# Six norms with fewer sums on TensorE, and another order of a gather's first head, in a two-block decoder kernel

## The reference

```python
def rmsnorm(x, g):
    ms = jnp.mean(xf * xf, axis=-1, keepdims=True)
    return xf * lax.rsqrt(ms + EPS) * g
```

```python
s1, s2 = query_half_1 @ sub_keys1.T, query_half_2 @ sub_keys2.T   # 128 scores each
v1, i1 = top_k(s1, 16); v2, i2 = top_k(s2, 16)
top_s, pos = top_k(v1[:, None] + v2[None, :], 16)                 # 16 of 256 pairs
eidx = i1 * 128 + i2 at pos;  g = softmax(top_s)
a = gelu(expert_down[eidx] . x)                                   # 16 rows of 1024
out += (g * a) @ expert_up[eidx]                                  # 16 rows of 1024
```

## Time and profile before

| what | value |
|---|---|
| median of 3 runs | 1639.43 us (1639.33 to 1641.08) |
| profiled execution, its own time | 1639.54 us |
| its span in the trace | 1637.8 us |
| mean granted TensorE clock | 0.898 of full |
| busy: PE / DVE / ACT / POOL | 81% / 59% / 21% / 30% |
| DMA in the mean | 238 GB/s, 389.75 MB |
| chain that ended last | PE 53%, DMA 26%, DVE 12%, POOL 4% |

### The profile page before, as it was taken

How to read it: one execution, slowest core, us unless ns; L and a number is a source line. 1 busy time by engine, 2 the same in 40 slices (tenths; PEclk the granted TensorE clock), 3 DMA queues, 4 the chain that set the end, 5 groups by cost and what they waited for, 6 DMA issues and landing times.

```text
span 1637.8 us, 14570 instructions
## 1 busy us (share of the span) xinstructions
PE 1332.4 (81%) x5214; PEld 936.5 (57%) x5214; DVE 959.0 (59%) x1851; ACT 338.5 (21%) x677; POOL 493.6 (30%) x390
## 2 busy tenths in 40 slices
PE   7999999999999999999999987565566656555554
PEld 5665668888888888886787776222222222222221
DVE  7799974123311000323412168898988998988977
ACT  2444222321100000122312122111111121111111
POOL 2477670000000000000000024755555555555550
PEclk9999999999999999999999998877777777877776
DMA  6222222244344444322242377999999999999995
GB/s 238 77 78 77 78 103 103 103 157 177 128 149 148 150 145 153 128 103 103 77 143 91 117 303 288 405 422 421 422 422 421 422 422 421 422 422 422 421 422 211
DMA packets 55150, 389.75 MB, mean 238 GB/s; under 512 B 6336, under 2 KB 6656, under 8 KB 8368
## 3 DMA queue, kind: packets, MB, share of 16 engines
q0 software_dynamic: 37488, 271.20, 40.1%
q1 hardware_dynamic: 16560, 115.48, 19.7%
q10 hardware_dynamic: 1040, 2.26, 0.4%
HBM read 387.88 MB, written 1.05 MB: 237 GB/s over the span
## 4 chain that ended last, share of the span: by engine, by line
PE 53%; DMA 26%; DVE 12%; POOL 4%; issue 2%; ACT 2%; ACTq 0%; DVEq 0%
DMA feat<-in_expert,arena 26%; PE psD L930 16%; PE psD L978 7%; PE psD L384 7%; PE psD L881 6%; POOL feat L1782 4%; PE psD L949 3%; PE psD L1288 1%; DVE feat L1795 1%; PE psN L313 1%; DVE arena L619 1%; DVE feat L1829 1%; DVE feat L537 1%; PE psD L874 1%; PE psD L575 1%
## 5 line engine op out<-in xcount | busy, mean ns | idle before, releaser
L930 PE MATMUL psD<-feat,ring 128*128 128x256 f32 (+1 forms) x1248 | 278.1, 383 | 4.4 <-DVE feat L338 3.2
L930 PEld LDWEIGHTS psD<-feat,ring 128*128 128x128 f32 x1248 | 238.6, 192 | 39.1 <-issue 4.5
L1782 POOL DMA_INDIRECT arena<-in_expert,arena x102 | 140.0, 1373 | 208.7 <-DVE arena L1762 53.0
L1970 POOL DMA_DIRECT2D arena<-in_sub x1 | 0.6, 577 | 525.2 <-ACT feat L1504 525.2
L881 PE MATMUL psD<-feat,ring 128*128 128x256 f32 (+1 forms) x576 | 138.1, 396 | 3.0 <-ACT feat L916 3.0
L1795 DVE CUSTOM_DVE_ANT_0 arena<-arena,feat 128x1024 f32<-128x1024 f32 x102 | 120.7, 1220 | 12.8 <-DMA arena<-in_expert,arena 12.8
L881 PEld LDWEIGHTS psD<-feat,ring 128*128 128x128 f32 x576 | 109.2, 194 | 30.5 <-issue 10.5
L1619 PE MATMUL psB<-arena 128*128 128x512 f32 x96 | 73.2, 923 | 64.1 <-ACT arena L1694 64.1
L1782 POOL DMA_INDIRECT feat<-in_expert,arena x77 | 107.7, 1398 | 57.9 <-DVE feat L1829 17.0
L978 PE MATMUL psD<-feat,ring 128*128 128x256 f32 x512 | 111.2, 379 | 0.0
L384 PE MATMUL psD<-feat,ring 128*128 128x256 f32 x512 | 110.8, 379 | 0.0
(11 more groups left out here) (501 smaller groups left out, 2203.1 us busy)
## 6 DMA issues: line engine op xcount, KB each, us to landing
ring<-in_w SPq DMA_DIRECT2D x108, 1024.0 KB, 4.8
arena<-in_expert,arena POOLq DMA_INDIRECT x102, 27.1
feat<-in_expert,arena POOLq DMA_INDIRECT x77, 28.7
feat<-in_xT SPq DMA_DIRECT2D x2, 544.0 KB, 4.6
arena<-in_w_akv POOLq DMA_DIRECT2D x1, 1024.0 KB, 5.2
feat<-in_memT POOLq DMA_DIRECT2D x1, 1024.0 KB, 5.9
out<-feat SPq DMA_DIRECT2D x4, 256.0 KB, 4.7
ring<-in_expert,arena POOLq DMA_INDIRECT x60, 28.7
```

The source lines that it names most:

```text
L930: mm = nc.tensor.matmul(psD[:, 2 * (c % 2) + m, 0:T], ring[:, c % RING, k, m * P:(m + 1) * P], x[:, k], start=(k == 0), stop=(k == KT - 1))
L1782: (nc.gpsimd.indirect_dma_start(GPAIR[b], None, a["expert"], bass.IndirectOffsetOnAxis(ap=EID[:, t, c:c + 1], axis=0)) .then_inc(s_gb[b], 16))
```

## The change

It has three parts.

- **Norms 2 to 7.** `squares_dve(i)` adds, on DVE, the squares of blocks 2 and 3 to those of blocks 0 and 1, and then those of blocks 4 and 5. `sums_pe(i)` is now one call of four matmuls (blocks 0, 1, 6, 7) at the place where the last pair stood; the spread pairs are gone.
- **First head.** Its four calls of `coefficients` move from behind the heads (3, 5, 6, 7) to behind (2, 4, 5, 7). Row i of step 0 takes buffer `SOON[i % 9]` of `[2, 3, 4, 12, 13, 14, 15, 0, 1]`. So (1, 0) to (1, 4) wait for (0, 7) to (0, 11), (1, 5) to (1, 11) for the last scores, (1, 12) to (1, 15) for (0, 12) to (0, 15).
- **Last step.** `both` moves from behind group 2 to behind group 1; group 2's own rows (8 and 10) are added into `ACC` one after the other; `close(1)` also waits for row (15, 10).

```diff
-SOON = 9
+SOON = [2, 3, 4, 12, 13, 14, 15, 0, 1]
...
-    def sums_pe(i, j):
-        nc.tensor.wait_ge(s_sqp, 4 * (i - 2) + j + 1)
-        if j == 0:
-            nc.tensor.wait_ge(s_rt, i)
-        for k in (2 * j, 2 * j + 1):
-            mm = nc.tensor.matmul(psN[:, 0:T2], ones[:, :], SQ[:, k, 0:T2], start=(k == 0), stop=(k == KT - 1))
-        if j == 3:
-            mm.then_inc(s_ms, 1)
+    def squares_dve(i, link):
+        for j in (1, 2):
+            nc.vector.wait_ge(s_sqp, 4 * (i - 2) + j + 1)
+            ins = nc.vector.tensor_tensor(SQ[:, 0:2, 0:T2], SQ[:, 0:2, 0:T2], SQ[:, 2 * j:2 * j + 2, 0:T2], ALU.add)
+            if j == 1:
+                link(ins)
+        ins.then_inc(s_sqa, 1)
+
+    def sums_pe(i):
+        nc.tensor.wait_ge(s_rt, i)
+        nc.tensor.wait_ge(s_sqa, i - 1)
+        for k in (0, 1, 6, 7):
+            if k == 6:
+                nc.tensor.wait_ge(s_sqp, 4 * (i - 2) + 4)
+            mm = nc.tensor.matmul(psN[:, 0:T2], ones[:, :], SQ[:, k, 0:T2], start=(k == 0), stop=(k == 7))
+        mm.then_inc(s_ms, 1)
...
-                if kg == 2 and mg:
-                    sums_pe(4, mg - 1)
...
+    soon = [carve([2 * D]) for _ in range(6)] + [VT[:, 0:2].rearrange("p a d -> p (a d)"), slot(SQ), slot(ZS)]
+    late = [slot(feat[:, i]) for i in (1, 3, 4)] + [slot(ring[:, j]) for j in range(RING)]
+    GPAIR = [soon[SOON.index(i)] if i in SOON else late.pop(0) for i in range(PTOP)]
...
-        return i % SOON if g == 0 else i
+        return SOON[i % len(SOON)] if g == 0 else i
...
-            if h in (3, 5, 6, 7):
-                coefficients(0, (3, 5, 6, 7).index(h))
+            if h in (2, 4, 5, 7):
+                coefficients(0, (2, 4, 5, 7).index(h))
...
-                if g == 0 and i >= SOON:
-                    nc.gpsimd.wait_ge(*used(0, i - SOON))
-                if g == 1 and i < SOON:
-                    nc.gpsimd.wait_ge(*used(0, i + SOON if i + SOON < PTOP else i))
-                if g == 1 and i == SOON:
+                if b in last:
+                    nc.gpsimd.wait_ge(*used(*last[b]))
+                elif g:
                     nc.gpsimd.wait_ge(s_ps, PH + 1)
-                if g > 1:
-                    nc.gpsimd.wait_ge(*used(g - 1, i))
+                last[b] = g, i
...
-            closed = g == 2 * PH - 1 and q >= 3
+            closed = g == 2 * PH - 1 and q >= 2
...
+            if t:
+                dve.wait_ge(s_usev, NUP[2 * PH - 1, 10])
...
-                if g == PH - 1 and q == 3 or g == 2 * PH - 1 and q == 2:
+                if g == PH - 1 and q == 3 or g == 2 * PH - 1 and q == 1:
                     both(g, q)
...
+        squares_dve(2, link)
         postnorm_dve(2, YSF, FIRST["w_out"], 1, "g_mix_post", link, mark)
+        squares_dve(3, link)
...
+        squares_dve(4, link)
         postnorm_dve(4, ZSF, FIRST["w_ff2"], 4, "g_ffn_post", link, mark)
+        squares_dve(5, link)
...
         add_dve("w_out_2")
+        squares_dve(6, link)
...
         add_dve("xo")
+        squares_dve(7, link)
...
             chunk_pe(FIRST["w_out"], j, RRB, T2)
-            sums_pe(2, j - 1)
-        sums_pe(2, 3)
+        sums_pe(2)
         chunk_pe(FIRST["xk0"], 0, MEM, T2, fresh=2)
-        sums_pe(3, 0)
-        sums_pe(3, 1)
...
+        chunk_pe(FIRST["xk0"], 1, MEM, T2, mid=lambda: sums_pe(3))
...
-            if j:
-                sums_pe(6, j - 1)
-        tok_pe(FIRST["xvb"], 0, MEM, mid=lambda: sums_pe(6, 3))
+        tok_pe(FIRST["xvb"], 0, MEM, mid=lambda: sums_pe(6))
...
             chunk_pe(FIRST["xo"], j, OX, T2)
-            if j:
-                sums_pe(7, j - 1)
-        sums_pe(7, 3)
+        sums_pe(7)
```

More of the change, by code:

```diff
@@ L1058, in build @@
     slot = lambda v: v.rearrange("p k t -> p (k t)")[:, 0:2 * D]
-    GPAIR = [carve([2 * D]) for _ in range(6)] + [VT[:, 0:2].rearrange("p a d -> p (a d)"), slot(SQ), slot(ZS)]
-    assert len(GPAIR) == SOON
-    GPAIR += [slot(feat[:, i]) for i in (1, 3, 4)] + [slot(ring[:, j]) for j in range(RING)]
+    soon = [carve([2 * D]) for _ in range(6)] + [VT[:, 0:2].rearrange("p a d -> p (a d)"), slot(SQ), slot(ZS)]
+    late = [slot(feat[:, i]) for i in (1, 3, 4)] + [slot(ring[:, j]) for j in range(RING)]
+    GPAIR = [soon[SOON.index(i)] if i in SOON else late.pop(0) for i in range(PTOP)]
     assert len(GPAIR) == PTOP
@@ L1538, in pair @@
     def pair(g, i):
-        return i % SOON if g == 0 else i
+        return SOON[i % len(SOON)] if g == 0 else i
     def filled_pair(g, i):
         if g == 0:
-            return i // SOON + 1
-        return g + sum(j % SOON == i for j in range(PTOP))
+            return i // len(SOON) + 1
+        return g + sum(pair(0, j) == i for j in range(PTOP))
     def used(g, i):
@@ L1765, in gathers_pool @@
     def gathers_pool():
+        last = {}
         for g in range(2 * PH):
@@ L2213, in _ @@
         ff2_pe(FFH, T2)
[L2214 removed]
+        sums_pe(4)
         chunk_pe(FIRST["xk1"], 0, MEM, T2, clear=FIRST["w_ff2"] + 12)
[L2216 to L2218 removed]
+        chunk_pe(FIRST["xk1"], 1, MEM, T2, mid=lambda: sums_pe(5))
         for j in range(4):
```

9 lines of the change are left out of this document (1 added, 8 removed).

## The result

| | before | after |
|---|---|---|
| median of 14 runs, taken by turns on one chip | 1640.6 us (1639.1 to 1644.7) | 1620.43 us (1616.2 to 1633.7) |
| profiled execution, its own time | 1639.54 us | 1620.72 us |
| span, mean granted clock | 1637.8 us, 0.898 | 1619.0 us, 0.901 |

The ratio is 0.9891, with a 95% interval of 0.9868 to 0.9915: faster by 1.1%, 5.3 us above the forecast of 1615.1. The runs of the changed kernel lie in two groups, nine from 1616.2 to 1620.8 us and five from 1628.9 to 1633.7, with nothing in between. The kernel before has no second group. In the nine the mean granted TensorE clock is 0.900 to 0.910, in the five 0.893 to 0.898. The profiled execution is one of the nine. The median of the nine alone is 1618.45 us, so of the 5.3 us above the forecast 2.0 come from the second group and 3.4 are in the first as well.

A forecast was written before the change was run, and what follows sets the result against it. PE was taken to bound the first half, the gathers (DMA) the second. From 1639.54 us, 9.8 (norms), 13.5 (first head) and 1.1 (tail) were subtracted, giving 1615.1 us; range 1612 to 1622.

The forecast's parts named there:

- Part 1: Norms 2 to 7: fewer matmuls on PE save 9.8 us, all of it reaching the first gather.
- the step to the first gather: Between norms and gathers: every later stage hangs on the norms, so all 9.8 us should arrive.
- Norm 7: Last merged norm: 1.73 us saved, but DVE's additions (+0.7) and two more matmuls (+0.86) leave 0.2 us gain.
- Rival D: Slower than before: PE idles at merged sums, its clock halves for the following chunk, 6.9 us each; 1643 us, chance 0.02.
- Part 2: First head: earlier gelus and new buffer order close the gaps in the gathers, worth 13.5 us.
- the nameless idle time: Before head 2's evacuation ACT idled 9.43 us, released by nothing the trace can name.
- rival A: Last scores come late through a stall like ACT's behind a full queue: 1618 to 1622 us, chance 0.15.
- the tightest spot: Row (1, 5), waiting for the last scores, could land at 1019.7 against its turn at 1020.3: 0.6 us to spare.
- The list of stalls: Gathers after the change: no stall of POOL before step 2 but the one for the last scores.
- Part 3: Tail: `both` moves into DVE's wait for row (15, 10), gaining 1.1 us.
- B: Only norms and tail pay, gaps move on as DVE becomes the pace: 1628.6 us; with other partial closings chance 0.12.
- C: DVE's additions come behind PE in norms 3, 5 and 7, losing 4.5 us: 1619.6 us, chance 0.08.

The follow-up runs named there:

- e6_padded: Changed kernel with two unread matmuls in place of each pair removed from norms 2 to 5: 1625.33 us, ratio 0.9933.
- e10_one_block: Changed kernel with 18 unread matmuls in one block in front of the projection ahead of the attention stage: 1625.28 us, ratio 0.9895.
- e14_merged_plus_three: Changed kernel with norm 7 in its old form and three unread matmuls in front of the projection ahead of attention: 1615.64 us, ratio 0.9879.
- e13_six_products: Changed kernel with the old norms and six unread matmuls in front of the projection ahead of attention: 1630.44 us, ratio 0.9974.
- e1_norms: Kernel before with only the six merged norms, first head and last step as before: 1630.98 us, ratio 0.9982.
- e5_changed_again: Changed kernel unaltered, run again on another chip: 1629.35 us, ratio 0.9929.
- e15_changed_third: Changed kernel unaltered, run a third time on another chip: 1620.16 us, ratio 0.9918.

## Why the prediction was right or wrong

- **Part 1, the terms: right.** Norms 2 to 5 gave 7.8 us (forecast 7.8) and norm 6 gave 1.7 (1.73). Norm 7 was to gain 0.2 and lost 0.4 to 0.55. The two additions and two matmuls were counted at full clock, but the matmuls behind the gap ran at half (3.15 us for 1.9).
- **Part 1, the step to the first gather: wrong. This is the step that failed:** "Every later stage hangs on it, so all of it should reach the first gather." It supposes that a stage keeps its length when it begins earlier. The attention stage does not: the same instructions take 80.8, about 84, or 94.8 us, according to what the clock does in it. Where part 1 puts it, 21 of 50 runs fall in the second group, and the three of them that were profiled lose 14.0 us in the stage. `e6_padded` and `e10_one_block` show that merging without the shift makes no such group, `e14_merged_plus_three` and its two repetitions that 1.3 us of delay take it out. Whether the shift makes one without merging too is open: `e13_six_products` had two such runs, but their clocks do not mark them as the same. In the lower groups part 1 did arrive for the most part: 7 to 9 us of the 9.8, an estimate from the medians (`e1_norms` 6.8 below before; `e5_changed_again` 18.2 and `e15_changed_third` 17.2, less the 9.4 of parts 2 and 3 from another chip).
- **The 6.1 us missing in the profiled execution:** 3.0 are the clock, 0.6 norm 7, and 2.5 a start that came out worse in it. The first and the last are executions more than kernels: I priced from one profile of before in which the stage stayed at 2.4 GHz, and three of six profiles with the old stream ahead of the stage have 84.1. There the fall was partly given back (from the stage's start to the first gather 224.2 us against 223.5), since the dip in the cross attention was missing and norm 7's next chunk took 7.11 us instead of 8.34.
- **Rival D named the mechanism at the wrong place.** I looked for the half clock behind new gaps of PE, where only norm 7 had one, and found it cheap. It came in a stage of which the diff says nothing and the profile of before showed a clock of 1.00, and it hung on where that stage begins, not on gaps at the norms.
- **Part 2: the mechanism right, the size only where before has the nameless idle time.** The gaps closed to 416 GB/s, and 13.8 us came (10.5 at row (1, 11), 3.3 in the steps) for 13.5. But the 13.5 were priced from one execution of before, whose first gelu was some 5 us late by the very idle time that I discussed only as a danger to the new order (rival A). On a chip without it parts 2 and 3 together bring 9.4 us. That 15.1 came for 14.6 was luck to that extent: before and the changed kernel were compared on a chip that has the idle time. The last scores, the tightest spot, were on time to 0.2 us. The list of stalls was wrong (four instead of one), which cost nothing.
- **Part 3:** 1.1 forecast; 1.2 in the changed kernel, 0.2 alone, since the price left out that `close(1)` also waits for PE.
- **B and C** did not happen: DVE worked its lag off, and the additions were ready at each norm but 7, where the wait was forecast.
- **Open.** What the clock's control takes as a reason to fall, and why one and the same PE stream shows the fall of 3.3 us in one execution and not in another, no run here can tell. Nor is there a rule for good places: earlier by 6.4 us or later by 6.9 was harmless as to the second group, earlier by 7.8 was not, and later by 2.6 is unsettled. The Trainium skill, "TensorE: Matmul & The Clock Gate", What's actually happening, says that the gate's measuring runs freely and is not reset when a kernel starts, and that the same kernel therefore shows different numbers of slow matmuls in different executions. The two groups of one program, and starts that differ by 2.5 us, agree. What released ACT in the 9.4 us is open as well: no row names it, and nothing was tried that could.

## What to carry to other kernels

Time saved on an engine is not time saved at the end if a stage behind it changes its length. Here it was a stage with thin matmuls in it, by the clock. So compare the granted clock of every stage that is moved, edited or not, in more than one profile of either kernel, and try the change with a microsecond or two of idle work ahead of that stage (here 1.3 us of it brought 4.5 in the median). Look at all the run times and not at their median alone: two groups can be a mechanism, and a profile shows only one of them. Check by their clocks whether two such groups are the same thing. And before pricing a gap, see whether the execution that it is read from holds a stall that has no name; it may belong to the chip and not to the kernel.

## What was not expected of the hardware

- The attention stage, 80.8 us at 2.4 GHz, takes 83.8 to 84.1 with one dip to 1.2 GHz of about 7 us and 94.8 with one of 30 us. The same PE stream had 80.8 in three profiles and 84.1 in three. PE was busy 3.8 us and 4.0 us of 4 in the two low windows shown.
- Full products set between the four-row ones did not hold the clock: 97.4 us, with 34.1 us at 1.2 GHz.
- ACT stood idle for 9.4 to 10.8 us ahead of one evacuation, with the DMA queue newly full, in every trace from some chips and in none from others; the kernel before takes 1640.6 and 1640.9 us there and 1635.3 to 1636.5 elsewhere.
